# 42 sparse tokens in three slot groups with whole gathered rows; V's low weights on VectorE, one of twelve of U's too

## What is computed

```python
u = jnp.take(expert_u, eb, axis=0)                  # rows of (16384, 2048)
act = gelu(einsum('tkd,td->tk', u, xb))
v = jnp.take(expert_v, eb, axis=0)
y = einsum('tk,tkd->td', gb * act, v)
out = rmsnorm(x + y)
```

## Time and profile before

| | us |
|---|---|
| median of 3 executions | 1913.71 |
| range | 1912.99 to 1914.73 |
| span of the profiled execution | 1912.2 |
| front | 0 to about 571 |
| U | 571 to 1251 |
| V | 1254 to 1899 |
| tail | 1899 to 1912 |

### The profile page before, as it was taken

The page is one execution under the profiler, slowest core; times in us unless marked ns, Lnnn a source line. Parts: engine busy times, 40 slices in busy tenths (PEclk is TensorE's granted clock), DMA queues, the critical chain, the costliest instruction groups (busy, mean ns, idle before and its releaser), DMA issues.

```text
span 1912.2 us, 35061 instructions
## 1 busy us (share of the span) xinstructions
PE 1896.7 (99%) x11798; PEld 1758.9 (92%) x11798; DVE 1383.4 (72%) x2585; ACT 950.5 (50%) x1342; POOL 1390.8 (73%) x708
## 2 busy tenths in 40 slices
PE   9999999999999999999999999999999999999997
PEld 7888889888999999999999999999999999999997
DVE  7534684045545777968888888479889889999986
ACT  6453355475544444544444444455555555555555
POOL 3867768887998999998888888976555525666711
PEclk9999999999999999999999999999999999999999
DMA  8544546564655666666666566689999988999984
GB/s 307 186 143 153 199 144 224 193 190 155 218 188 177 207 209 208 210 202 196 194 192 196 189 195 195 200 280 351 333 336 334 333 297 298 337 325 334 328 273 145
DMA packets 128380, 448.29 MB, mean 234 GB/s; under 512 B 16528, under 2 KB 19472, under 8 KB 127632
## 3 DMA queue, kind: packets, MB, share of 16 engines
q1 hardware_dynamic: 102240, 367.29, 58.5%
q0 software_dynamic: 20480, 67.13, 10.0%
q10 hardware_dynamic: 5584, 12.88, 2.0%
HBM read 443.04 MB, written 4.19 MB: 234 GB/s over the span
## 4 chain that ended last, share of the span: by engine, by line
PE 72%; POOL 17%; issue 8%; DMA 1%; DVE 1%; ACT 0%; POOLq 0%; SPq 0%; DVEq 0%; ACTq 0%
PE ps L1885 22%; PE ps L1982 22%; POOL wlo L438 17%; PE ps L1888 12%; PE ps L1985 11%; PE ps L1899 1%; PE ps L1585 1%; PE ps L1587 1%; PE ps L1586 1%; PE ps L1961 1%; DMA raw<-in_w_front 0%; PE ps L1869 0%; DMA big<-in_x_t 0%; PE ps L1963 0%; ACT whi L539 0%
## 5 line engine op out<-in xcount | busy, mean ns | idle before, releaser
L438 POOL TENSOR_TENSOR wlo<-raw,whi 128x1024 fp32r<-128x1024 f32 x436 | 1057.6, 2430 | 207.9 <-ACT whi L539 193.1
L539 ACT ACTIVATE whi<-raw 128x1024 fp32r<-128x1024 f32 x435 | 461.2, 1060 | 633.7 <-PE ps L1888 361.8
L1885 PE MATMUL ps<-x_parts,whi 128*128 128x448 f32 x2048 | 588.9, 369 | 0.0
L1982 PE MATMUL ps<-gate_parts,whi 128*128 128x448 f32 x1992 | 573.6, 369 | 0.0
L734 ACT ACTIVATE whi<-raw 128x1024 fp32r<-128x1024 f32 x256 | 271.7, 1061 | 294.9 <-PE ps L1985 255.8
L1888 PEld LDWEIGHTS ps<-x_parts,wlo 128*128 128x128 f32 x2048 | 384.7, 188 | 31.3
L1985 PEld LDWEIGHTS ps<-gate_parts,wlo 128*128 128x128 f32 x1992 | 374.2, 188 | 30.8
L1888 PE MATMUL ps<-x_parts,wlo 128*128 128x224 f32 x2048 | 386.9, 270 | 0.0
L1985 PE MATMUL ps<-gate_parts,wlo 128*128 128x224 f32 x1992 | 376.0, 270 | 0.0
L1437 DVE TENSOR_TENSOR wlo<-raw,whi 128x1024 fp32r<-128x1024 f32 x248 | 303.9, 1225 | 68.1 <-ACT whi L734 52.1
L1885 PEld LDWEIGHTS ps<-x_parts,whi 128*128 128x128 f32 x2048 | 310.3, 191 | 0.0
(11 more groups left out here) (266 smaller groups left out, 2217.2 us busy)
## 6 DMA issues: line engine op xcount, KB each, us to landing
raw<-in_w_u SPq DMA_DIRECT2D x256, 512.0 KB
raw<-in_w_v SPq DMA_DIRECT2D x256, 512.0 KB
raw<-in_w_front SPq DMA_DIRECT2D x180, 512.0 KB
big<-in_mem ACTq DMA_DIRECT2D x8, 256.0 KB, 5.6
big<-in_mem_t ACTq DMA_DIRECT2D x2, 1024.0 KB, 6.2
big<-in_x ACTq DMA_DIRECT2D x2, 1024.0 KB, 7.3
x_back<-x2t_scratch ACTq DMA_DIRECT2D x2, 896.0 KB
big<-in_x_t SPq DMA_DIRECT2D x3, 512.0 KB, 8.4
```

The source lines that it names most:

```text
L438: nc.gpsimd.tensor_tensor(wlo[:, j % SPL, :], raw[:, j % RAW, :], whi[:, j % SPL, :], ALU.subtract).then_inc(lo_done, 1)
L539: nc.scalar.activation(whi[:, j % SPL, :], raw[:, j % RAW, :], ACT.Copy).then_inc(hi_done, 1)
L1885: nc.tensor.matmul(sums[:, 0:2 * TD], whi[:, s, cols], x_parts[:, :, m, 0:TD], start=m == 0, stop=False, skip_group_check=True)
L1982: nc.tensor.matmul(sums[:, 0:2 * TD], whi[:, s, cols], gate_parts[:, g, :, 0:TD], start=False, stop=False, skip_group_check=True)
```

## The change

- The sparse tokens go from 32 to 42 (TS = 128 // 3), the dense ones from 224 to TD = 214. The wide matmuls have 428 columns and the narrow ones 214, their number is the same, and there are 107 pairs of tokens for the gates.
- Gathered rows are whole (2048 values, 8 KB). The 128 partitions hold 3 groups of 42 tokens, each with a third of the 128 slots (PER = 43), so there are 43 + 43 gathers of 128 rows, 1 MB each, in place of 128 + 128 of 256 KB. The ring has 3 slots. V's rows come from a table of their own.
- U rows are taken in pieces 15 to 118, V rows in pieces 128 to 232 (`taken`). The first three gathers are issued behind pieces 3, 4 and 5 of V (`issued`), between GpSimd's last low splits.
- No fold on TensorE: each partition's sum is whole. The three groups' results are added at the end instead, after DMAs that bring them to the same partitions (`load_addend`, `add_group`, pieces 240, 241, 251), and the sum of squares is taken at piece 252.
- x for the sparse tokens is loaded three times (once a group), and the gain is broadcast to 128 partitions.
- In U, piece 10 of each body of 12 gets its low part from VectorE, behind the join of pieces 6 and 7 (21 pieces). V's split stays as it was, GpSimd for the first 8 pieces and VectorE for the rest.

```diff
-TD, TS, PARTS, PD = 224, 32, 4, 512
+GROUPS = 3
+TS = P // GROUPS
+TD = T - TS
+PER = -(-P // GROUPS)
 TOK_PAIRS = TD // 2
-RING = 12
+RING = 3
 ACT_BANKS = 3
-POOL_END = V0 + 8
-FOLD_BODY, LAST_ROWS = 10, 242
+FOLD_BODY = 10
 OPENING, SPARE_BLOCKS, VECTOR_LOW = 8, 5, 8
...
-def issued_u(d):
-    return OPENING if d < RING else taken_u(d - RING) + 1
-
-
-def taken_u(d):
-    return 15 + d * 41 // 50
-
-
-def issued_v(e):
-    return 117 + e if e < RING else taken_v(e - RING) + 1
-
-
-def taken_v(e):
-    return 132 + e * 21 // 25
+ROWS_FROM, WEIGHTS_AT_PIECE, ROWS_UNTIL = 15, 127, 234
+ADDED_AT = (*range(240, 239 + GROUPS), 251)
+
+
+def taken(n):
+    if n < PER:
+        return ROWS_FROM + n * (WEIGHTS_AT_PIECE - 6 - ROWS_FROM) // PER
+    return WEIGHTS_AT_PIECE + 1 + (n - PER) * (ROWS_UNTIL - WEIGHTS_AT_PIECE) // PER
+
+
+def issued(n):
+    return 3 + n if n < RING else taken(n - RING) + 2
+
...
+U_VECTOR = 10
+U_BODIES = 2 * NK // BODY
+LOW_V0 = V0 - U_BODIES
...
+            if j == U_VECTOR and not (isinstance(i, int) and i == U_BODIES):
+                return lo_u_done, i + 1
+            return lo_done, i * (BODY - 1) + (U0 + j + (j < U_VECTOR))
...
+            if isinstance(i, int) and i == 0 and j < OPENING:
+                return lo_done, LOW_V0 + j + 1
+            return lo_v_done, i * BODY + (j - OPENING + 1)
...
+            with pool.Fori(U0 // BODY, U0 // BODY + U_BODIES) as i:
+                for j in range(BODY):
+                    if j != U_VECTOR:
+                        rest_of(i * BODY, j)
+            for j in range(RAW):
+                rest_of(U0 + U_BODIES * BODY, j)
...
+            def gather(n):
+
+                if n < RING:
+                    pool.wait_ge(used, V0)
                 else:
-                    pool.wait_ge(used, V0 + 4 + d)
-                gather(d % RING, u_rows, IDX[0][:, d:d + 1])
-
-            def gather_v(e):
-
...
+                    pool.wait_ge(rows_taken, n - RING + 1)
+                nc.gpsimd.indirect_dma_start(ROW[n % RING], None, u_rows if n < PER else v_rows,
+                                             bass.IndirectOffsetOnAxis(IDX[:, n % PER:n % PER + 1].bitcast(I32), 0)
+                                             ).then_inc(row_in[n % RING], 16)
+
+            asked = 0
+            for j in range(2 * NK):
+                if j < OPENING:
+                    rest_of_v(j)
+                if j == 3:
                     pool.wait_ge(picks, 1)
-                    pool.wait_ge(used, V0)
-                while asked[0] < P and j >= issued_u(asked[0]):
-                    gather_u(asked[0])
-                    asked[0] += 1
-                while asked[1] < P and j >= issued_v(asked[1]):
-                    gather_v(asked[1])
-                    asked[1] += 1
-            assert asked == [P, P]
+                while asked < 2 * PER and j >= issued(asked):
+                    gather(asked)
+                    asked += 1
...
-                for p in range(PARTS):
-                    part, cols = slice(p * TS, (p + 1) * TS), slice(p * PD, (p + 1) * PD)
-                    if j == 3:
-                        act.dma_start(X_S[part, :], x2_dram[:, cols]).then_inc(x_s_in, 16)
-                    if j == 6:
-                        act.dma_start(GAIN_S[part, :], gain_rows[0, cols].partition_broadcast(TS)).then_inc(gain_s_in, 16)
-                    if j == 9:
-                        act.dma_start(LAST_GAIN_S[part, :], gain_rows[1, cols].partition_broadcast(TS)).then_inc(last_gain_s_in, 16)
+                if j == 3:
+                    for g in range(GROUPS):
+                        act.dma_start(X_S[g * TS:(g + 1) * TS, :], x2_dram).then_inc(x_s_in, 16)
+                if j == 6:
+                    act.dma_start(X_GAINED, gain_rows[0].partition_broadcast(P)).then_inc(gain_s_in, 16)
...
-                if j == 2:
-                    act.wait_ge(folded, 1)
-                    nc.scalar.activation(WEIGHTS.rearrange("p (a b) -> p a b", a=2), ps[:, 0:2, 2 * TD:512], ACT.Gelu,
-                                         scale=PICK_R).then_inc(sparse_gelu, 1)
...
+                if j == 5:
+                    act.wait_ge(rows_taken, PER)
+                    nc.scalar.activation(WEIGHTS, SUMS, ACT.Gelu, scale=PICK_R).then_inc(sparse_gelu, 1)
...
+                if j == 8:
+                    act.wait_ge(rows_taken, 2 * PER)
+                    load_addend(0)
+                    load_addend(1)
...
+                if j == 3:
+                    for k in range(2, GROUPS):
+                        act.wait_ge(group_added, k - 1)
+                        load_addend(k)
+                    act.wait_ge(group_added, GROUPS - 1)
+                    act.dma_start(ADDEND[GROUPS], gain_rows[1].partition_broadcast(TS)).then_inc(last_gain_s_in, 16)
...
+                if c % CHUNKS_PER_BODY == U_VECTOR // 2 - 2:
+                    n = 2 * c + 4
+                    dve.wait_ge(hi_done, k0 * 2 + (U0 + n + 1))
+                    nc.vector.tensor_tensor(wlo[:, (U0 + n) % SPL, :], raw[:, n % RAW, :], whi[:, (U0 + n) % SPL, :],
+                                            ALU.subtract).then_inc(lo_u_done, 1)
...
+            def row_taken(n):
+                dve.wait_ge(row_in[n % RING], 16 * (n // RING + 1))
+                row, k = ROW[n % RING], n % PER
+                weight = WEIGHTS[:, k:k + 1]
+                if n < PER:
+                    ins = nc.vector.tensor_tensor_reduce(row, row, X_GAINED, 1.0, 0.0, ALU.mult, ALU.add, SUMS[:, k:k + 1])
+                elif k == 0:
+                    ins = nc.vector.tensor_scalar(X_GAINED, row, weight, None, ALU.mult)
+                else:
+                    dve.wait_ge(rows_taken, n)
+                    ins = nc.vector.scalar_tensor_tensor(X_GAINED, row, weight, X_GAINED, ALU.mult, ALU.add)
+                ins.then_inc(rows_taken, 1)
+
+            def add_group(k):
+
+                dve.wait_ge(group_in[k], 16)
+                if k:
+                    dve.wait_ge(group_added, k)
+                nc.vector.tensor_tensor(Y_S, Y_S, ADDEND[k], ALU.add).then_inc(group_added, 1)
...
-                v_step(j, split=V0 + j >= POOL_END)
+                v_step(j, split=j >= OPENING)
...
-                    dve.wait_ge(x_s_in, 16 * PARTS)
-                    dve.wait_ge(gain_s_in, 16 * PARTS)
-                    step(nc.vector.tensor_tensor(X_GAINED, X_S, GAIN_S, ALU.mult))
...
+                    dve.wait_ge(x_s_in, 16 * GROUPS)
+                    dve.wait_ge(gain_s_in, 16)
+                    filled = slice(0, GROUPS * TS)
+                    step(nc.vector.tensor_tensor(X_GAINED[filled], X_S[filled], X_GAINED[filled], ALU.mult))
...
-                while done[1] < P and j >= taken_v(done[1]):
-                    v_row(done[1])
-                    done[1] += 1
...
+                while done < 2 * PER and j >= taken(done):
+                    row_taken(done)
+                    done += 1
+                if j in ADDED_AT:
+                    add_group(ADDED_AT.index(j))
+                if j == 252:
+                    dve.wait_ge(group_added, GROUPS)
+                    step(nc.vector.tensor_tensor_reduce(ADDEND[GROUPS - 1], Y_S, Y_S, 1.0, 0.0, ALU.mult, ALU.add,
+                                                        stats[0:TS, SPARSE_R:SPARSE_R + 1]))
+                    nc.vector.tensor_scalar(stats[:, VAR + N_LAST:VAR + N_LAST + 1], stats[:, SPARSE_R:SPARSE_R + 1], 1.0 / D, EPS,
+                                            ALU.mult, ALU.add).then_inc(var_ready, 1)
+            assert done == 2 * PER
...
-            dve.wait_ge(last_gain_s_in, 16 * PARTS)
-            nc.vector.scalar_tensor_tensor(X_GAINED, X_S, stats[:, R + N_LAST:R + N_LAST + 1], LAST_GAIN_S,
+            dve.wait_ge(last_gain_s_in, 16)
+            nc.vector.scalar_tensor_tensor(Y_S, Y_S, stats[0:TS, R + N_LAST:R + N_LAST + 1], ADDEND[GROUPS],
...
-            for k, src in enumerate((CH[:, 0, last], CH[:, 1, last], GE[:, last], stats[:, R + N_X2 + 1:R + N_X2 + 2])):
-                w = P if k < 3 else 1
-                ins = nc.tensor.matmul(ps[:, 7, k * P:k * P + w], SEL, src, start=True, stop=True)
+            for k, src in enumerate((CH[:, 0, last], CH[:, 1, last], GE[:, last])):
+                for g in range(GROUPS):
+                    w = min(PER, P - g * PER)
+                    nc.tensor.matmul(ps[:, 7, k * PER:k * PER + w], SEL[:, g, :], src[:, g * PER:g * PER + w],
+                                     start=g == 0, stop=g == GROUPS - 1, skip_group_check=True)
+            for g in range(GROUPS):
+                ins = nc.tensor.matmul(ps[:, 7, 3 * PER:3 * PER + 1], SEL[:, g, :], stats[:, R + N_X2 + 1:R + N_X2 + 2],
+                                       start=g == 0, stop=g == GROUPS - 1)
```

283 lines of the change are left out of this document (121 added, 162 removed).

## The result

The changed kernel takes **1945.43 us** (median of 4 runs, 1943.44 to 1946.53) against 1913.35 before (4 runs beside them): a ratio of 1.0168, 95% interval 1.0153 to 1.0182. It is 1.7% slower; 1902 was forecast, and a range that ended at 1930. The profiled execution spans 1944.7 us against 1912.2, 32.5 us more.

The account below looks back on a forecast made before the run. TensorE was taken to set the pace, with the DMA engines close behind in V and becoming the bound there. Terms -19.2 - 1.2 - 0.5 + 2.8 - 3.3 + 6 + 1.5 + 1 + 1.5 = -11.4 us gave 1902; range 1872 to 1930.

Parts of the forecast that it names:

- TensorE's piece: U and V: wide matmuls shrink, narrow ones stay at 0.105 us; a piece goes from 2.52 to 2.445 us.
- A cost by columns: TensorE's lower bound: wide and narrow matmuls both shrink with their columns, 2.407 us a piece.
- Gates, fold and picks: TensorE: 5 fewer gate pairs give -1.2 us; fold, norm and pick matmuls together -0.5 (-1 to +1).
- Low split in U: VectorE's 21 splits in U: nil, up to +3 us; without them GpSimd would hold U at about 2.49 a piece.
- V's DMA term: V's 212 pieces with gathers: DMA engines bind at 375 GB/s, 2.533 us a piece, +2.8 us (-15.9 to +26.7).
- Rival 2: V: DMA engines bind lower and it gets slower; 359 GB/s gives 1926 us, 348 gives 1944; chance 0.25.
- Rival 1: V: DMA engines don't bind, V gains 19.2 us as U does; 1881 us, or 1861; chance 0.22.
- VectorE in V: V: longer rows fill VectorE to 93 to 96%, in lumps, but fit; costed at nil.
- Opening: V's first pieces: larger early loads and gathers, and GpSimd's queue, cost +6 us (+3 to +9).
- Pieces 127 to 131: Middle of V: the row of piece 128 stands ahead of `first_block` on VectorE; +1.5 us (0 to 2.2).
- The adds: End of V: adds of 2.2 us in pieces 240, 241, 251 and the squares at 252; +1 us.
- The tail: After V: L1540 grows from 0.75 to 2.3 us right ahead of the last eight joins; +1.5 us.

Follow-up runs that it names:

- e_u_eight: The changed kernel with VectorE's one split of 12 in U moved from the eleventh piece of a body to the ninth: 1935.6 us, ratio 1.0113.
- e_u_pool: The changed kernel with all of U's low-weight splits on GpSimd, as before the change, V as changed: 1928.6 us, ratio 1.0085.
- e_dense: The changed kernel with half rows in V, U's splits all on GpSimd, and the first table's rows over 92 pieces instead of 106: 1900.0 us, ratio 0.9935.
- e_v_half_bytes: The changed kernel with gathers of only the first 1024 columns of each row, row instructions at full length: 1922.7 us, ratio 1.0039.
- e_v_halves: The changed kernel with each row fetched and used as two halves of 1024 columns, six half buffers for three: 1908.9 us, ratio 0.9968.
- e_v_no_gather: The changed kernel with the first three gathers only, all row instructions at full length: 1909.0 us, ratio 0.9974.

## Why the prediction was wrong

**TensorE's piece: right.** 2.445 forecast, 2.453 measured, by the step that was named: the wide matmuls shrink (0.42 to 0.40 for two), the narrow ones stay at 0.21 for two. That it is the weight load that holds them was the prediction's reading of the earlier trace rows; no run here changed the weight load by itself. A cost by columns (2.407 us a piece, the lower bound) would have shrunk both; the narrow pair still takes 0.21 (700.43 to 700.64). Gates, fold and picks: nil to -2, as said.

**Low split in U: the step that failed first.** It was costed at nil to +3 us, because VectorE works 511 of 680 us and its waits could take 21 splits. It cost 15.5 us. Idle time was counted over the stage and not at the place. In a body with gates VectorE's waits didn't cover the step that got the split (moved by two pieces it cost nothing there, e_u_eight), and what is queued behind the split (`hot_row`) holds TensorE; in the search there is no idle time, and the split took 2.6 times its own length beside GpSimd. The prediction named "where the search makes a join late", and sized it at 3 us; measured are 4.9 us there (pieces 81 to 83), of which 2.0 are the wait for the late low part and 2.9 the half clock behind it, a cost that the prediction had nowhere; and 10.6 us are in the bodies with gates, which it didn't name. The other half of this step was also wrong: "without that edit it would be" the bound at 2.49. In e_u_pool GpSimd's split takes 2.433 on average and the pieces 2.453. The 14.95/6 of the earlier trace rows was in V's opening.

**Search and picks.** Even without the split, pieces 79 to 82 and 95 take 4 us more than before (3.70, 2.55, 3.36, 2.55 and 5.70 against four times 2.52 and 3.99): VectorE's long steps stay as they are while TensorE comes sooner. Of TensorE's gain in U, 17 us by 256 x 0.067, they give back 4. This loss wasn't in the sum. Half of it is chance: in e_dense and e_v_half_bytes pieces 79 to 82 take 2.45 to 2.56 us.

**V's DMA term: right sign, wrong mechanism, too small.** The 213 pieces lost 18.0 us, not 2.8. The forecast took a capacity, 375 GB/s, and divided. The runs show that the capacity was at least 405, that the same bytes in half rows cost next to nothing (e_v_halves: excess 2.8), and that whole rows cost 30 us at a mean rate below it. So the step that failed is the division by a capacity: the pieces went to 555.2 / 213 = 2.61 us on average through stalls of single pieces, with weights landing late and long row instructions in their way. Rival 2's price for them (359 GB/s, 2.646 us a piece) is near that, which is luck: its rate was an effect and not a cause. Rival 1 ("the DMA engines don't bind") had the capacity right and the time wrong. The core moved 388 and 405 GB/s over 190 us each (e_v_halves, e_dense), above the 359 and 348 that spoke for rival 2.

**VectorE in V: half right.** The lumps cost nothing by themselves (e_v_no_gather), as costed. What was missing, as the traces read, is that the same lump takes its length from the room of the weight load four pieces on, and frees a row buffer in the same moment. Terms that were each covered were summed as if their covers were independent.

**Opening, middle, end.** Opening +6.4 against +6 less 1.2 for the narrower pieces: near, with some luck. Pieces 6 and 7 run at a granted clock of 0.50 for 3.4 us, behind a wait of 3.29 us, which costs 1.7 that weren't in the sum. Pieces 127 to 131 +1.7 against 1.1: the same, 3.4 us at half clock behind piece 128's stall; three executions of the same rows without it (e_u_eight, e_v_no_gather, e_v_half_bytes) take 15.0 us there, +0.7. The adds: +0.7 against -0.7. The tail +3.0 against +1.5: the same kind of row as before is now

```profile
1925.15 2.34 DVE L1589 SCALAR_TENSOR_TENSOR big<-big,stats,gather_low 42x2048 f32<-42x2048 f32 x1
1927.42 4.16 DVE L1523 TENSOR_REDUCE big<-ps 128x214 f32<-128x428 f32 x8
```

1.6 us longer as forecast; the rest of the 3.0 I have not traced.

Of the 43 us between 1902 and 1945, then, U's split holds 15.5, the rest of U 7, V's gathers 15, the small places 6. Some 6 of these 43 are half clock behind stalls: 2.9 in U, 1.7 in the opening and about 1 at piece 129.

## What to carry to other kernels

Idle time of a second engine counts only at the place in its order where the new work goes (here 21 splits of 1.22 us cost 15.5 us where 134.6 us of waits for TensorE had been counted): ask what is queued right behind it and who waits for that. Buffers that are each late by less than their slack are not safe together when the same instruction frees both; cut the long instruction and the long transfer together (excess 2.8 us here, against 32.6 and 39.6 for one of them alone), and judge by TensorE's piece times, not by another engine's wait. A rate measured while the consumer stalls is not a capacity (366 GB/s here with TensorE idle for 7 of 190 us, 388 and 405 with no idle time). And look at the granted clock behind each long stall of TensorE: the stall may be less than half of the loss (2.0 of 4.9 us in pieces 81 to 83).
